# Output gate multiplied into the mixing product on VectorE instead of into the weights on GpSimd, with the first tile's operands loaded in the stage ahead

## What is computed

```python
def mixer_output(p, y_ssd, grid, pool_w, pool_scale, ssd_norm_w, w_out):
    y_pool = pool_mixer(u_pool, pool_w, pool_scale, grid) * jax.nn.silu(z_pool)
    gated = (y_ssd * jax.nn.silu(z_ssd)).reshape(bsz, n, SSD_GROUPS, W_SSD // SSD_GROUPS)
    y_s = rmsnorm(gated, ssd_norm_w.reshape(SSD_GROUPS, W_SSD // SSD_GROUPS)).reshape(bsz, n, W_SSD)
    return jnp.concatenate([y_pool, y_s], axis=-1) @ w_out
...
        h_lat = h_lat + g_l * mixer_output(p_lat, y_ssd_lat, True, pool_w[i], pool_scale[i],
                                           ssd_norm_w[i], w_out[i])
...
    return rmsnorm(h_lat, final_norm_w)
```

## Time and profile before

| | us |
|---|---|
| median of 3 runs | 3387.61 |
| lowest and highest run | 3380.34, 3389.07 |
| the profiled execution, its own time | 3380.37 |
| its span in the trace | 3378.5 |
| granted TensorE clock, mean of the span | 0.968 |
| TensorE matmul busy | 3167.3 (94% of the span) |
| VectorE busy | 1618.8 (48%) |
| ScalarE busy | 968.0 (29%) |
| GpSimd busy | 343.3 (10%) |

### The profile page before, as it was taken

One profiled execution on the slowest core, in us unless ns is written; L12 is line 12 of the kernel. 1 busy time (PEld: TensorE's weight loads), 2 busy tenths in 40 slices (PEclk: granted clock), 3 DMA queues, 4 the chain that ended last, 5 costly groups with the idle time before them and its releaser, 6 DMA issues. The chain is left out here.

```text
span 3378.5 us, 37778 instructions
## 1 busy us (share of the span) xinstructions
PE 3167.3 (94%) x14940; PEld 2512.8 (74%) x14940; DVE 1618.8 (48%) x1907; ACT 968.0 (29%) x1784; POOL 343.3 (10%) x181
## 2 busy tenths in 40 slices
PE   8999999998999969978999969999999799999898
PEld 8788888876888847767888858888877455555577
DVE  4645543576024436875444443243343565554365
ACT  4422221101211116633222231233223334433310
POOL 0000000000022213552000000000000201000012
PEclk9999999998999979998999989999999699999899
DMA  6122323432246665754333342222123412210242
GB/s 216 44 61 64 115 85 128 153 109 88 83 165 203 221 182 191 241 188 139 124 118 112 112 159 66 89 99 94 56 94 99 97 39 51 63 38 7 94 131 100
DMA packets 213150, 381.47 MB, mean 113 GB/s; under 512 B 18826, under 2 KB 140426, under 8 KB 205093
## 3 DMA queue, kind: packets, MB, share of 16 engines
q1 hardware_dynamic: 193382, 347.47, 31.6%
q10 hardware_dynamic: 17296, 26.88, 2.3%
q0 software_dynamic: 2336, 5.21, 0.7%
HBM read 250.29 MB, written 129.08 MB: 112 GB/s over the span
## 5 line engine op out<-in xcount | busy, mean ns | idle before, releaser
L670 PE MATMUL p_ps<-hmT_hi,p_w_hi 128*128 128x512 f32 x1312 | 525.5, 401 | 15.9 <-ACT p_work L375 13.0
L670 PE MATMUL p_ps<-hmT_lo,p_w_hi 128*128 128x512 f32 x1312 | 512.1, 390 | 0.0
L670 PE MATMUL p_ps<-hmT_hi,p_w_lo 128*128 128x512 f32 x1280 | 500.4, 391 | 0.0
L1757 PE MATMUL p_ps<-h2T_hi,p_w_hi 128*128 128x512 f32 x800 | 326.8, 408 | 24.0 <-DVE h2T_lo L1614 24.0
L1757 PE MATMUL p_ps<-h2T_lo,p_w_hi 128*128 128x512 f32 x800 | 313.7, 392 | 0.0
L670 PEld LDWEIGHTS p_ps<-hmT_hi,p_w_hi 128*128 128x128 f32 x1312 | 247.5, 189 | 71.7 <-issue 17.6
L1757 PE MATMUL p_ps<-h2T_hi,p_w_lo 128*128 128x512 f32 x768 | 300.0, 391 | 0.0
L670 PEld LDWEIGHTS p_ps<-hmT_lo,p_w_hi 128*128 128x128 f32 x1312 | 247.5, 189 | 49.3
L670 PEld LDWEIGHTS p_ps<-hmT_hi,p_w_lo 128*128 128x128 f32 x1280 | 241.0, 188 | 51.8
L1919 PE MATMUL t_psO<-t_prob,t_v 128*65 128x512 f32 (+3 forms) x640 | 260.5, 529 | 0.9 <-DVE t_out_turned L2029 0.2
L1976 ACT ACTIVATE t_prob<-t_psS 128x1024 f32<-128x1024 f32 (+1 forms) x160 | 150.0, 938 | 307.8 <-PE t_psS L1907 177.6
(11 more groups left out here) (375 smaller groups left out, 5732.6 us busy)
## 6 DMA issues: line engine op xcount, KB each, us to landing
p_w_raw<-in_w_in SPq DMA_DIRECT2D x66, 512.0 KB, 6.0
p_spare<-scratch_xs_tok SPq DMA_DIRECT2D x34, 512.0 KB, 4.4
p_spare<-in_wada ACTq DMA_DIRECT2D x32, 512.0 KB, 5.7
scratch_xs_tok<-p_work SPq DMA_DIRECT2D x8, 1152.0 KB
p_work<-scratch_b_tok SPq DMA_DIRECT2D x34, 256.0 KB, 5.0
p_work<-in_wada SPq DMA_DIRECT2D x16, 512.0 KB, 4.5
p_work<-in_x SPq DMA_DIRECT2D x16, 512.0 KB, 3.7
scratch_dT<-p_work SPq DMA_DIRECT2D x8, 1024.0 KB, 5.9
```

The lines of the kernel that those rows point to most:

```text
L670: mm = pe.matmul(PS[:, c, 0:width], wt[n][:, q, :], xx[:, q, cols], start=(q == 0 and j == 0), stop=(q == KT - 1 and j == len(terms) - 1))
L1757: mm = pe.matmul(ps[:, c, :], wt[n][:, q, :], xx[:, q, c * CH:(c + 1) * CH], start=(q == 0 and j == 0), stop=(q == KT - 1 and j == len(ter ...
```

## The change

The gate row is no longer multiplied into the weights. GpSimd's 8 products in the scan block and its 8 in the mixing block are gone, and ScalarE makes the high parts straight from the loaded piece. In its place VectorE's `residual` has two instructions for each half: the product psMix times gate row into `rt`, then `rt` plus x. A new semaphore `gated` is raised by the first; TensorE now waits for it (not for `r`) before it overwrites the half of psMix, and the second VectorE instruction waits for it too.

The three operand buffers `m_d`, `m_zp` and `m_g`, with their semaphores, are now allocated around both blocks, and their loads for tile 0 are issued by SyncE in the scan block, behind the pooling weights, instead of at the head of the mixing block.

```diff
@@ scan block, SyncE, in the turn of chunk 14
                         sp.dma_start(w.pool[:], a["pool_w"]).then_inc(w.pool_in, 16)
+                        tiles = lambda t: t[:].rearrange("p (k n) -> p k n", n=P)
+                        sp.dma_start(tiles(w.d), cols_at(a["dT"], 0)).then_inc(w.d_in, 16)
+                        sp.dma_start(tiles(w.zp), cols_at(a["zpT"], 0)).then_inc(w.zp_in, 16)
+                        sp.wait_ge(y_out[0], 16)
+                        sp.dma_start(w.g[:], tokens(a["g_tok"], 0)).then_inc(w.g_in, 16)
@@ scan block, GpSimd
-                    if c == 1:
-                        g.wait_ge(S["gate_in"], 16)
-                    if c % 2 == 1:
-                        g.wait_ge(S["w_in"], 16 * (c // 2 + 1))
-                        g.tensor_tensor(piece[:], piece[:], w.gate[:], ALU.mult).then_inc(S["w_gated"], 1)
@@ scan block, ScalarE
-                        act.wait_ge(S["w_gated"], q + 1)
+                        act.wait_ge(S["w_in"], 16 * (q + 1))
@@ mixing block, SyncE
-                load(0)
                 for q in range(EARLY, MT):
@@ mixing block, ScalarE
-                    act.wait_ge(S["scaled"], q - EARLY + 1)
+                    act.wait_ge(p_in[q % 4], 16 * ((q - EARLY) // 4 + 1))
@@ mixing block, VectorE, residual(t, q)
-                    v.tensor_tensor(rt[:, q * CH:(q + 1) * CH], psM[:, q, :], xt[:, q * CH:(q + 1) * CH],
-                                    ALU.add).then_inc(S["r"], 1)
+                    cols = slice(q * CH, (q + 1) * CH)
+                    v.tensor_tensor(rt[:, cols], psM[:, q, :], w.gate[:, cols], ALU.mult).then_inc(S["gated"], 1)
+                    v.wait_ge(S["gated"], 2 * t + q + 1)
+                    v.tensor_tensor(rt[:, cols], rt[:, cols], xt[:, cols], ALU.add).then_inc(S["r"], 1)
@@ mixing block, VectorE, ahead of the first tile
+                v.wait_ge(w.gate_in, 16)
@@ mixing block, GpSimd
-            @block.gpsimd
-            def _(g_):
-                for q in range(EARLY, MT):
-                    g_.wait_ge(p_in[q % 4], 16 * ((q - EARLY) // 4 + 1))
-                    g_.tensor_tensor(piece[q % 4][:], piece[q % 4][:], w.gate[:], ALU.mult).then_inc(S["scaled"], 1)
@@ mixing block, TensorE, half(t, n, h)
-                        pe.wait_ge(S["r"], 2 * t + h - 1)
+                        pe.wait_ge(S["gated"], 2 * t + h - 1)
```

More of the change, by code:

```diff
@@ L786, in ssd @@
                           "merged", "decays", "inside", "off_f", "off_f_read", "forward", "off_b", "off_b_read", "summed_y",
-                          "gated", "const", "zeros", "lndt_in", "rows_in", "gate_in", "masks_in", "const_in", "seg_in", "z_in", "w_in", "w_gated", "w_hi",
+                          "gated", "const", "zeros", "lndt_in", "rows_in", "masks_in", "const_in", "seg_in", "z_in", "w_in", "w_hi",
                           "w_lo"))
@@ L819, in _ @@
                 load_hb(1)
-                sp.dma_start(w.gate[:], a["gate_rows"][0:1, :].partition_broadcast(P)).then_inc(S["gate_in"], 16)
+                sp.dma_start(w.gate[:], a["gate_rows"][0:1, :].partition_broadcast(P)).then_inc(w.gate_in, 16)
                 sp.wait_ge(S["cb"], 1)
@@ L1080, in mix_out @@
         fnorm = sb("final_norm_row", [P, D])
-        dt_, zp, g, xt = (sb(n, [P, D]) for n in ("m_d", "m_zp", "m_g", "m_x"))
+        dt_, zp, g, xt = w.d, w.zp, w.g, sb("m_x", [P, D])
         y_hi, y_lo = [sb("m_y_hi0", [P, MT, P], F32R)], [sb("m_y_lo0", [P, MT, P], F32R)]
@@ L1097, in mix_out @@
         k = kit
-        S = k.sems("m_", ("rows_in", "scaled", "w_hi_ok", "w_lo_ok", "ssq", "root4", "gs", "yp", "hi_p", "hi_g", "lo_p", "lo_g",
+        S = k.sems("m_", ("rows_in", "w_hi_ok", "w_lo_ok", "ssq", "root4", "gs", "yp", "hi_p", "hi_g", "lo_p", "lo_g",
                   "pool", "turn_g", "turn_h", "half", "r", "sq", "root", "x1", "mv", "root2", "hn", "ev_a", "ev_v",
-                  "d_in", "zp_in", "g_in", "x_in", "x1_out", "h2_out", "sum_ok"))
+                  "x_in", "gated", "x1_out", "h2_out", "sum_ok"))
         p_in = [k.sem(f"m_piece_loaded{n}") for n in range(4)]
@@ L1108, in load @@
                         sp.wait_ge(S["pool"], t)
-                    sp.dma_start(tiles(dt_), cols_at(a["dT"], t)).then_inc(S["d_in"], 16)
+                    sp.dma_start(tiles(dt_), cols_at(a["dT"], t)).then_inc(w.d_in, 16)
                     if not starts(t):
                         sp.wait_ge(S["lo_p"], t)
-                    sp.dma_start(tiles(zp), cols_at(a["zpT"], t)).then_inc(S["zp_in"], 16)
+                    sp.dma_start(tiles(zp), cols_at(a["zpT"], t)).then_inc(w.zp_in, 16)
                     if not starts(t):
                         sp.wait_ge(S["turn_g"], t)
-                    sp.dma_start(g[:], rows_at(a["g_tok"], t)).then_inc(S["g_in"], 16)
-                load(0)
+                    sp.dma_start(g[:], rows_at(a["g_tok"], t)).then_inc(w.g_in, 16)
                 for q in range(EARLY, MT):
@@ L1149, in squares @@
                 def squares(t):
-                    act.wait_ge(S["g_in"], 16 * (t + 1))
+                    act.wait_ge(w.g_in, 16 * (t + 1))
                     if not starts(t):
@@ L1212, in operands @@
                     v.wait_ge(S["pool"], t + 1)
-                    v.wait_ge(S["zp_in"], 16 * (t + 1))
+                    v.wait_ge(w.zp_in, 16 * (t + 1))
                     v.tensor_tensor(tiles(zp), psP[:], tiles(zp), ALU.mult).then_inc(S["yp"], 1)
@@ L1283, in front @@
                 def front(t, n):
-                    pe.wait_ge(S["d_in"], 16 * (t + 1))
+                    pe.wait_ge(w.d_in, 16 * (t + 1))
                     if not starts(t):
@@ L2404, in program @@
             w.pool, w.pool_in = kit.sbuf(out, "pool_w_sb", [P, 4, 2, 256]), kit.sem("pool_w_loaded")
+            w.d, w.zp, w.g = (kit.sbuf(out, n, [P, D]) for n in ("m_d", "m_zp", "m_g"))
+            w.d_in, w.zp_in, w.g_in, w.gate_in = (kit.sem(f"m_{n}_loaded") for n in ("d", "zp", "g", "gate"))
             ssd(nc, kit, a, s, w)
```

## The result

| | median us | runs | profiled execution us | its span us |
|---|---|---|---|---|
| before, measured beside it | 3382.52 | 5 (3379.99 to 3389.07) | 3380.37 | 3378.5 |
| after | 3365.39 | 5 (3359.92 to 3368.82) | 3368.82 | 3366.8 |

The ratio is 0.9939, with a 95% interval of 0.9927 to 0.9950: 17 to 25 us less, where 14.1 were forecast. A later pair of runs, 5 of the changed kernel beside 20 of the kernel before, gave 3364.15 against 3384.48, 0.9938 (0.9925 to 0.9952). So the gain is too large for the prediction, and the question is where the rest comes from. Times inside a kernel (block, stage, starts) are those of its one profiled execution, medians those of all its runs.

The account below looks back on a forecast made before the run. TensorE bounds both blocks, so gain lies only in the poor stretches between: profiled 3380.37 - 14.8 + 0.7 = 3366.3; for the median 3387.6 - 14.1 = 3373.5 us, range 3363 to 3380.

Parts of the forecast that it names:

- First tile: Head of the mixing block: TensorE starts at 1515.7, first half at about 1526.0, 8.7 us earlier than 1534.65.
- TensorE starts late: Rival, head of the mixing block: TensorE not ready at 1515.7, up to 4.4 us of gain lost, 3378; chance 0.10.
- Late weights and second tile: Mixing block: fifth piece issued 9.5 us earlier, g lands 14.6 us later, half 1 of tile 0 starts 14.8 us earlier.
- Scan block: Block ahead of mixing: dropping GpSimd's products and adding three loads costs 0, with up to 1 us of gain.
- VectorE in the steady tiles: Mixing block: added VectorE instruction costs 0 in 15 tiles; rival, VectorE becomes the bound, 3394.5, chance 0.04.
- tail +0.7: After the mixing block's last half: one more VectorE instruction has no cover there, costing 0.7 us.
- The rest of the program: Everything outside the scan and mixing blocks: given no term in the sum, so taken as unchanged.
- -14.8: Mixing block: term for half 1 of tile 0 starting at 1546.3 instead of 1561.1.
- The level: Whole kernel: starting median of 3387.6 us, to which the forecast gain of 14.1 us was applied.

Follow-up runs that it names:

- after_again: The changed kernel, unchanged, timed again beside the kernel before: 3364.15 us, ratio 0.9938.
- prefetch_only: The kernel before with only tile 0's three loads moved into the scan block, the gate still multiplied into the weights on GpSimd: 3377.25 us, ratio 0.9976.
- seven_pieces: The changed kernel with seven buffers instead of four for the late weights' pieces, seven issued at the block's start: 3360.90 us, ratio 0.9924.
- before_turns: The kernel before with one wait more: VectorE's low-part product in the attention stage waits for GpSimd's t_spare of that head: 3378.30 us, ratio 0.9979.

## Why the prediction was right and wrong

The mechanism in the two blocks was right; the sum was wrong because it took the rest of the program as unchanged. That the median, 3365.4, still lies in the stated 3363 to 3380 is luck: the gains behind that range were 8 to 17 us, the measured one is 17 to 25, and only the lower edge, set at the level of the fastest run, takes it in.

In the block, each from its first load:

| step | before | forecast | measured |
|---|---|---|---|
| TensorE's first matmul | 4.5 | 0.1 | 0.2 |
| first half of tile 0 | 19.0 | 10.4 | 10.8 |
| fifth piece issued | 21.2 | 11.7 | 11.9 |
| half 1 of tile 0 | 45.5 | 30.7 | 30.95 |
| length | 473.6 | -14.1 | -13.8 |

- *First tile.* Right, by its own steps: squares and normed g ended under the cover of TensorE's pooling (1519.91 + 1.22 = 1521.1, ahead of 1522.3), then pooled product, high part, two low parts of 1.22 us each. The pooled low part fell from 3.36 to 1.22 us with GpSimd idle. Of that the Trainium skill (SBUF — State Buffer, section "SBUF: two separate sides") says that VectorE and GpSimd share a pair of ports that one of them holds for a whole instruction while the other is blocked; the trace agrees: before, the low part began 0.08 us behind a product of GpSimd and ended 1.1 us behind that product's end (1532.4 and 1533.5).
- *TensorE starts late.* This rival, 0.10, falls: its first matmul starts 0.19 us behind SyncE's first load of the block, and the same in after_again, prefetch_only and seven_pieces. No stall shows there.
- *Late weights and second tile.* Right in size: from the fifth piece's issue to the landing of g it took 14.4 us (14.6 kept). Inside, TensorE was less early than worked out: its pooling matmuls end at 1545.06, so 1.4 us ahead of the transposes instead of 2, since the last low part was late by about 1 us.
- *Scan block.* Priced at 0, and nothing shows there: SyncE's first load of the mixing block comes at 1516.34, 0.71 later, and the scan block's first matmul on `psSeg` 1.1 later (1247.3 and 1248.3). From that matmul to the mixing block's first load the other traces take 265 to 269 us with either kernel, so an effect under 1 us could not be seen.
- *VectorE in the steady tiles.* Right at 0, tail +0.7 (-14.5 at half 1, -13.8 at the end). The rival's point of decision, a pair that costs more than 0.69 + 2.97 us, was wrong: a set of 4.3 us costs the steady tiles nothing. What stands behind the pooled product's wait is further slack, from there to the next tile's first half.
- *The rest of the program.* **This step failed, and the prediction didn't put it as one.** Its sum runs from the profiled time with -14.8 and +0.7 and puts all else at nothing, without a reason. The attention stage got 7.0 us shorter (5.8 in the second trace of the changed kernel), by the order of two instructions that a longer VectorE list turned: before_turns, in which the order alone is changed, is 6.9 us shorter there. With it the sum is -13.8 - 7.0 = -20.8; the measured ratio of 0.9939 is -20.6 of 3382.5. No row of the profile before gives the size, but one told that something was there to be turned: a GpSimd instruction on one column that took 1.22 us at the median and 0.19 at best. Which way the place would fall could not have been worked out from it.
- *The level.* "For the median I take 3387.6 - 14.1" took three runs at their word. With 20 runs beside the other kernels the level is 3384.5, 3.1 less. That and the 6.7 that the gain was short make 3363.7 of 3373.5; measured were 3365.4. The sum from the profiled run, 3366.3, is near the result only by chance: with -20.8 it would be 3359.6, and the profiled run of the changed kernel took 3368.8, with 216.5 us from the last `t_psO` matmul to the last of the output, where the other traces have 208.9 to 214.2. One profiled run is no level either. What made that run's last stretch longer no experiment asked.

## What to carry to other kernels

Where two engines meet at a shared access within a tenth of a microsecond, an edit far upstream can turn the order, and with it what is issued behind them; look for an instruction whose median is several times its minimum, find its twin on the other engine, and write the order down with a wait if one of them stands on the path (here 0.55 us of VectorE's idle time in each of six heads bought 7 us). When a gain is larger than its mechanism, treat the surplus like a loss: cut the program into stages and compare their lengths before and after, and test the surplus by an edit that does no work. A cover is to be measured to the point where the bound engine really waits, not to the first idle time on the way.

## What the runs showed of the hardware

- A VectorE product with two inputs in SBUF (1.28 us) holds off a GpSimd instruction on one column that starts 0.11 us after it: 1.22 us instead of 0.19. Where GpSimd starts first, if only by 0.01 us, it takes 0.19 and the product its 1.28. The Trainium skill (SBUF — State Buffer, section "SBUF: two separate sides") states such a lock for a product with two SBUF inputs, and the trace agrees: `t_spare` ends 0.05 us behind the product. That a start shifted by 0.12 us turns the order, and that this can move 7 us of 3384, is what these runs add.
- The gap between two VectorE instructions depends on where they stand in the engine's list: the product starts 0.25 to 0.27 us behind the start of `t_max_lo` with 0, 4, 16 or 56 instructions more ahead of it, and with 8 more 0.61 in the first two heads of the loop and 0.37 in the other four. The mechanism is open.
- A transfer of 8 KB issued by GpSimd lands in 1.7 to 2.1 us in the heads in which it goes ahead of the 512 KB piece, in 1.7 in the one whose turn has no piece behind it, and in 3.4 to 3.9 when the piece is issued on another queue 0.35 us ahead of it.
